# Moving start-up loads behind the first weight panels, and context steps from the expert passes to the routers and seams

## The reference, cut to what matters

```
a, ac = modulate(h, ...), modulate(hc, ...)
y, yc = swa_mixer(a, ac, ...)            # layer 2, needs the context's own output
h  = h  + gt1 * y;    h  = h  + gt2 * swiglu(modulate(h), w_gate_up, w_down)
hc = hc + gt1c * yc;  hc = hc + gt2c * swiglu(modulate(hc), w_gate_up, w_down)
y, _ = na_mixer(a, modulate(hc), ...)    # layer 3, only keys and values of the context
```

## Time and profile before

| quantity | value |
|---|---|
| median of three runs | 2652.16 us |
| profiled execution | 2653.61 us |
| its span in the trace | 2651.7 us |
| PE busy | 2322.9 us (88%) |
| DVE busy | 769.1 us (29%) |
| ACT busy | 463.2 us (17%) |
| moved by DMA | 675.05 MB, mean 255 GB/s |
| mean granted PE clock | 0.939 |

### The profile page before, as it was taken

One profiled execution on the slowest core, in us unless ns is written; L12 is line 12 of the kernel. 1 busy time (PEld: TensorE's weight loads), 2 busy tenths in 40 slices (PEclk: granted clock), 3 DMA queues, 4 the chain that ended last, 5 costly groups with the idle time before them and its releaser, 6 DMA issues.

```text
span 2651.7 us, 29654 instructions
## 1 busy us (share of the span) xinstructions
PE 2322.9 (88%) x11896; PEld 1614.3 (61%) x11896; DVE 769.1 (29%) x1935; ACT 463.2 (17%) x1156; POOL 27.7 (1%) x43
## 2 busy tenths in 40 slices
PE   5977988888997579898989989659999999989999
PEld 3643854445663247485656546337678888568888
DVE  1135335422111120843212123136810003671000
ACT  1021113321000021320000021022710002351000
POOL 0000000000000000000000000000000000110000
PEclk8999989999998889999999999879899999899999
DMA  9799288859799974809887989972024443303430
GB/s 398 313 390 371 89 364 333 368 193 421 296 401 412 421 308 159 349 1 390 342 350 277 415 347 395 421 320 96 11 97 159 152 152 126 109 23 127 149 121 16
DMA packets 94053, 675.05 MB, mean 255 GB/s; under 512 B 10833, under 2 KB 10993, under 8 KB 12385
## 3 DMA queue, kind: packets, MB, share of 16 engines
q1 hardware_dynamic: 91296, 664.84, 62.1%
q0 software_dynamic: 2048, 5.21, 0.7%
q10 hardware_dynamic: 576, 3.15, 0.3%
HBM read 672.11 MB, written 1.05 MB: 254 GB/s over the span
## 4 chain that ended last, share of the span: by engine, by line
PE 71%; DMA 15%; DVE 9%; ACT 2%; issue 2%; SPq 1%; DVEq 0%; ACTq 0%
PE bank L760 69%; DMA ring<-in_moe_w 13%; DMA ring<-in_w_ada 1%; DMA ring<-in_even_w_out 1%; DVE work L2330 1%; DVE tiny L2318 1%; DVE work L1855 1%; ACT work L1381 1%; DVE scratch L1855 1%; PE bank L1266 1%; DVE work L2341 1%; ACT res L1381 0%; ACT u L1381 0%; SPq L692 0%; ACT scratch L1381 0%
## 5 line engine op out<-in xcount | busy, mean ns | idle before, releaser
L760 PE MATMUL bank<-u,ring 128*128 128x256 f32 x2912 | 649.8, 385 | 35.0 <-ACT u L1381 22.5
L760 PEld LDWEIGHTS bank<-u,ring 128*128 128x128 f32 x2912 | 561.7, 193 | 122.8 <-issue 32.7
L760 PE MATMUL bank<-ring,work 128*32 128x512 f32 (+2 forms) x2880 | 467.6, 678 | 127.5 <-DMA ring<-in_moe_w 115.5
L760 PEld LDWEIGHTS bank<-ring,work 128*32 128x32 f32 (+2 forms) x2880 | 142.3, 130 | 408.0 <-issue 404.4
L1381 ACT ACTIVATE work<-bank 128x256 f32<-128x256 f32 (+2 forms) x150 | 73.6, 491 | 1097.4 <-PE bank L760 884.6
L760 PE MATMUL bank<-scratch,ring 128*128 128x256 f32 x1120 | 257.7, 386 | 3.0 <-ACT scratch L1381 3.0
L760 PEld LDWEIGHTS bank<-scratch,ring 128*128 128x128 f32 x1120 | 212.0, 193 | 55.2 <-issue 23.8
L760 PE MATMUL bank<-work 128*128 128x128 f32 (+3 forms) x1216 | 221.4, 337 | 26.5 <-DVE work L2234 11.4
L760 PEld LDWEIGHTS bank<-work 128*128 128x128 f32 (+2 forms) x1216 | 179.6, 198 | 63.1 <-issue 26.5
L760 PE MATMUL bank<-work,ring 128*128 128x256 f32 x704 | 152.4, 379 | 2.5 <-DVE work L2364 2.5
L760 PEld LDWEIGHTS bank<-work,ring 128*128 128x128 f32 x704 | 133.6, 190 | 21.4 <-issue 3.3
(11 more groups left out here) (235 smaller groups left out, 1743.7 us busy)
## 6 DMA issues: line engine op xcount, KB each, us to landing
ring<-in_moe_w SPq DMA_DIRECT2D x360, 1024.0 KB, 15.4
ring<-in_w_ada SPq DMA_DIRECT2D x96, 1024.0 KB, 11.3
ring<-in_w_gate_up SPq DMA_DIRECT2D x44, 1024.0 KB, 6.9
ring<-in_w_down SPq DMA_DIRECT2D x23, 1024.0 KB, 5.5
ring<-in_ctx_gate_up SPq DMA_DIRECT2D x22, 1024.0 KB, 16.2
ring<-in_even_w_in SPq DMA_DIRECT2D x14, 1024.0 KB, 10.8
ring<-in_odd_w_in SPq DMA_DIRECT2D x12, 1024.0 KB, 19.5
ring<-in_na_w_qkv SPq DMA_DIRECT2D x12, 1024.0 KB, 4.8
```

The costliest lines, as they stand in the source:

```text
L760: return pe.matmul(o, l, r, start=start, stop=stop, skip_group_check=True)
```

## The change

The constants, x and the tables `first` were issued by ACT at once, behind `cols`. Now ACT waits until the fourth slot has landed, issues const and x, and issues `first` only after its own half of `modulate(0, 0)`. x has a semaphore of its own, and `first` is waited for where it is used (PE before `sbR`, DVE before `retS`). The fifth ada job of layer 0 moves ahead of the first projection panel, and every later one moves one panel forward.

The plans: the points outside the passes hold 28 steps instead of 18. route0b and route1b go from 3 to 4, ln0b from 2 to 4, and ln1b (4) and rms2a (2) are new. The passes of layer 0 hold 56 steps instead of 63 (8 4 9 4 9 4 10 8 instead of 9 5 10 5 10 5 13 6), those of layer 1 56 instead of 59 (8 4 8 4 8 4 9 11 instead of 9 4 9 4 9 4 10 10, as only ten were left for the last pass). For ln0b, ACT and DVE now run the context's part in `odd()`, behind `modulate(1, 0)`.

```diff
-CTX_PLAN = {"even": 2, "ln0a": 2, "route0a": 2, "route0b": 3, "ln0b": 2, "ln1a": 2, "route1a": 2, "route1b": 3}
-MOE_PLAN = (("111111111", "100111010", "111211111", "100111010", "111211111", "100111010", "212211112", "212100000"),
-            ("111111111", "100101010", "111111111", "100101010", "111111111", "100101010", "112111111", "334300000"))
+CTX_PLAN = {"even": 2, "ln0a": 2, "route0a": 2, "route0b": 4, "ln0b": 4, "ln1a": 2, "route1a": 2, "route1b": 4,
+            "ln1b": 4, "rms2a": 2}
+MOE_PLAN = (("011111111", "100101010", "111111111", "100101010", "111111111", "100101010", "112111111", "332000000"),
+            ("111111110", "100101010", "111111110", "100101010", "111111110", "100101010", "401011011", "443000000"))
...
         job("adafin0a", 1)
+        ada_jobs(0, 4, 5)
         for g in range(7):
             job(f"even.{g}", 2 if g in (2, 5) else 4, panel(a["even_w_in"][0], g))
-            ada_jobs(0, 4 + g, 5 + g)
+            ada_jobs(0, 5 + g, 6 + g)
             if g >= 3:
                 ada_jobs(1, g - 3, g - 2)
-        ada_jobs(0, 11, 12)
         job("adafin0b", 1)
...
             if L == 2:
+                ctx_jobs("rms2a")
+                assert not todo, todo
+                x_banks(ALL_BANKS)
...
                 ada_sums(0, "a")
-                pe.wait_ge(first_in, 32)
+                ada(0, 4, 5)
...
                     ada(1, 4 + 3 * b, 6 + 3 * b)
                     pe.wait_ge(sb_sp, b + 1)
+                    pe.wait_ge(first_in, 16)
...
             def second(L):
                 rms_sums(f"rms{L}a", RMS_N[L][0])
+                if L == 2:
+                    ctx("rms2a")
...
             def even():
                 modulate(0, 0)
+                act.dma_start(first, a["first"]).then_inc(first_in, 16)
...
             def odd():
                 modulate(1, 0)
+                ctx("ln0b")
...
                 layer_norm(f"ln{l}b", 2, l)
-                ctx(f"ln{l}b")
+                if l:
+                    ctx("ln1b")
...
             act.dma_start(cols[:, :], a["cols"]).then_inc(cols_in, 16)
-            act.dma_start(const[:, :], a["const"]).then_inc(const_in, 16)
-            act.dma_start(x, a["x"]).then_inc(first_in, 16)
-            act.dma_start(first, a["first"]).then_inc(first_in, 16)
             act.wait_ge(cols_in, 16)
             f(cond[:, :], cols[:, 0:24], ACT.Silu).then_inc(cond_done, 1)
+            act.wait_ge(loaded[loads[3][0]], 16)
+            act.dma_start(const[:, :], a["const"]).then_inc(const_in, 16)
+            act.dma_start(x, a["x"]).then_inc(x_in, 16)
             act.wait_ge(const_in, 16)
-            act.wait_ge(first_in, 32)
+            act.wait_ge(x_in, 16)
```

More of the change, by code:

```diff
@@ L551, in build @@
         ctx_jobs("ln1b")
-        assert not todo, todo
-        x_banks(ALL_BANKS)
         for L in (2, 3):
@@ L658, in build @@
         out_done = sem("output_stored")
-        dist_in = sem("distances_loaded")
+        dist_in, x_in = sem("distances_loaded"), sem("input_loaded")
         c_sq, c_cent, c_u = sem("ctx_squares"), sem("ctx_scaled"), sem("ctx_modulated")
@@ L959, in even @@
                         project(f"even.{g}", rhs, S)
-                    ada(0, 4 + g, 5 + g)
+                    ada(0, 5 + g, 6 + g)
                     if g >= 3:
                         ada(1, g - 3, g - 2)
-                ada(0, 11, 12)
                 ada_sums(0, "b")
@@ L1889, in even @@
                 dve.wait_ge(const_in, 16)
-                dve.wait_ge(first_in, 32)
+                dve.wait_ge(x_in, 16)
                 modulate(0, 0)
-                ada(0, 4, 5)
+                ada(0, 4, 6)
                 for i in range(4):
                     copy_tile(T("even.1", i), sk[:, i], S)
-                ada(0, 5, 6)
+                ada(0, 6, 7)
                 for i in range(2):
                     copy_tile(T("even.2", i), sv[:, i], 512)
-                ada(0, 6, 7)
+                ada(0, 7, 8)
                 for i in range(4):
@@ L1901, in even @@
                 for g in range(4):
-                    ada(0, 7 + g, 8 + g)
+                    ada(0, 8 + g, 9 + g)
                     ada(1, g, g + 1)
-                ada(0, 11, 12)
                 ada_sums(0, "b")
@@ L1927, in even @@
                     ada(1, 6 + 3 * b, 7 + 3 * b)
+                dve.wait_ge(first_in, 16)
                 for h in range(4):
```

## The result

The change made the kernel **0.38% faster**: a ratio of 0.9962 with an interval of 0.9949 to 0.9974. The median of twelve executions is 2646.62 us against 2654.58 for the kernel before. The profiled executions have spans of 2644.9 and 2651.7 us, so **6.8 us less where I had forecast 24.1**. The sign is right; the size is wrong, and the time lies just outside my range. (Three single executions taken for the later runs fell in a slow state, at 3523 to 8220 us; the ratios leave them out, and they move no median by more than 0.4 us.)

The account below looks back on a forecast made before the run. Neither PE nor the DMA stream alone bounds the expert passes; they alternate. Start 2.9, layer 0 22.0 and layer 1 7.0 saved, seams 4.6 and 3.2 lost: 24.1 us less, median 2628, range 2611 to 2646.

Parts of the forecast that it names:

- The start: Kernel start: first projection 1.0 us earlier and the fifth ada job inside its wait; 2.9 us saved, bounds 0 and 4.5.
- Routers and the seams: Routers' fourth step costs nothing, leaving 0.9 us idle; seam ln0b costs 4.6 us, ln1b and rms2a 3.2.
- Layer 0, passes 0 to 3: Pass 0 brings nothing; pass 2 loses a head step, passes 1 and 3 change little: 7.4 us saved, bounds 4 and 11.
- plus 1.8 as one of two slow phases [...] goes: Layer 0, pass 2: one of two phases taking 5 to 6 us instead of 3.6 disappears, saving 1.8 us.
- rival 3: In the passes, pauses left by thirteen removed steps slow next phases on the path; 17.6 us come back: 2646, chance 0.08.
- Rival 1: The stream binds every pass, so only slots leaving the passes count, 12.5 us: 2644.6, chance 0.14.
- Layer 0, passes 4 to 7: Gather 4 to phase 5 of pass 7 takes 238.7 us instead of 253.3: 14.6 saved, bounds 5 and 25.
- Layer 1, pass 0: The pass loses its s step, worth 3.5 us less the wait for DVE's sums it filled: 2.4 us saved.
- Layer 1, passes 4 and 5: Pass 4's ring no longer restarts at once: 116.2 us from gather 4 to gather 6 instead of 105.9, 10.3 lost.
- Layer 1, pass 6: The g steps' slot frees at once, the norm stands inside, one step fewer: 64.9 us instead of 75.1, 10.2 saved.
- more than 3 us: Sign of a wrong forecast: the norm's wait in pass 6 on the path with more than 3 us.
- Layer 1, pass 7: One slot fewer to phase 5, which was 59.8 us behind its gather: 2.3 us saved.

Follow-up runs that it names:

- the start alone: The kernel before with only the diff's changes of the start, the context plan left old: 2650.35 us, ratio 0.9979.
- an even clock: Kernels before and after compared with constant products filling PE's waits by one rule in both: 2642.16 us and 2622.88 us.
- first_pair_at_0: The kernel after with both steps of the first context slot at point 0, none at g, in layer 1's passes 0, 2 and 4: 2633.03 us.
- the last column: In a dropped table, what the change gave per stretch between kernels before and after with waits filled (2642.16 and 2622.88 us); sum 19.8 us.
- before_filled: The kernel before with constant products filling head waits and waits ahead of last phases in layers 0 and 1: 2642.16 us, ratio 0.9961.
- the filled kernels: The kernel after with waits filled and layer 1's first-slot steps moved in passes 0, 2, 4: 2613.27 us; with pass 6's norm sums also earlier: 2607.33 us.
- seams_taken_back: The kernel after with the six steps of ln1b and rms2a put back into layer 1's pass 7 at point 1: 2653.96 us, ratio 0.9989.
- plan_alone: The kernel before with all the diff's changes except those of the start: 2647.45 us, ratio 0.9968.

## Why the prediction was right and wrong

- **The start** was right in kind and forecast too small: 2.9 forecast, 4.0 found at the first gather, 4.2 for the start alone, of which 3.8 reached the end. A term was missed: with one ada row less ahead of the last sums, PE's wait of 1.29 us for DVE there (ahead of the product at 163.27 in the kernel before) is gone too. Over all traces kept the first gather comes at 351.2 us on average with the old start and 345.2 with the new, so 6 us may be nearer the truth, above my bound of 4.5.
- **Routers and the seams** were right: idle time 0.94 of 0.9; the seam ln0b costs 4.4 us behind the last scatter (31.66 instead of 27.23, forecast 4.6), ln1b and rms2a cost 3.1 (first 32 products ending 106.26 us behind the left-over gather). The left-over passes of layer 0 and layers 2 and 3 gave some 2.4 and 3.3 us back, which hid it in the bare total. The 3.3 are luck: over all traces the stretch behind the left-over gather takes 955.5 us with the old seam and 957.6 with the new, 2.1 more.
- **Layer 0, passes 0 to 3: the step that failed.** The count of steps, waits and tiles was right: at an even clock passes 1 to 3 gave 5.7 us, and my 7.4 without the slow phase is 5.6 (its parts 1.6, 2.4 and 1.5 make 5.5, where I wrote 5.7). Bare they gave 0.2. What failed was "plus 1.8 as one of two slow phases [...] goes" and, in the rivals, "I take most of these phases as hidden in the wait for the stream". Of the head waits of 2.39 or 3.91 us in passes 2 to 4, all six are followed by slow work in the kernel after, three of six in the kernel before, on PE's own path; and the last phase of pass 0, which was at 3.64, takes 6.31. I had seen this as rival 3, whose place is right and whose time, 2646, is what was measured; I gave it 0.08. Its price was partly luck: some 10 us come back at an even clock (16.9 - 6.8), not the 17.6 I worked out; most of the rest of the missing 17.3 us is layer 1's, below. Rival 1, at 2644.6, is as near to the measured time, and is wrong: it lets only the bytes count, and `first_pair_at_0` gained with the same bytes in passes 2 and 4.
- **Layer 0, passes 4 to 7**: 14.6 forecast, 10.9 found to phase 5 of pass 7, 12.7 at an even clock to the next gather. Pass 4 took 64.97 us (forecast 65) and pass 5 44.85 (44.0), phase 5 of pass 6 followed its gather by 54.9 (53) and that of pass 7 came 77.7 behind it (76.7). Pass 4 has its size, the others are a little short, the most pass 6, where the norm's wait of 3.27 us is followed by slow steps.
- **Layer 1, pass 0: a term missed**, 2.4 forecast and -3.0 found. I priced the lost s step at 2.4 and overlooked what I had written down for pass 4: that a g step in an old slot lets the ring restart at once. Up8 and up9 hold the first slot until step 0 ends, the eleven others are full before that, and the stream has a hole: from SP's first expert load to phase 5 it took 73.3 us (1187.63 to 1260.92) instead of 71.2 (1196.32 to 1267.55). The last phase is slow for 2.3 more. The 1.5 in the last column says little, as this pass is 1.1 us longer in `before_filled` than in the kernel before. With its slot free earlier the pass is 3.0 us shorter than in `first_pair_at_0`.
- **Layer 1, passes 4 and 5** were right to a tenth: -10.3. (A slot is 24.83 / 10 = 2.48 us, not 2.49; nothing hangs on it.) That a context slot at g and 0 holds the whole ring is shown by `first_pair_at_0`.

The timeline of the kernel after, passes 4, 6 and 7 of layer 1, against the earlier trace rows:

```profile
1435.09 3.81 PE L762 MATMUL bank<-work 128*128 128x128 f32 x32 [0.87 <-DVE work L2243]
...
1493.04 5.34 PE L762 MATMUL bank<-ring,work 128*32 128x512 f32 x32 [3.65 <-DMA ring<-in_moe_w]
...
1551.27 3.81 PE L762 MATMUL bank<-work 128*128 128x128 f32 x32 [0.87 <-DVE work L2243]
...
1594.90 6.29 PE L762 MATMUL bank<-scratch,ring 128*128 128x256 f32 x16 [6.16 <-ACT scratch L1385]
```

- **Layer 1, pass 6**: 10.2 forecast, 7.8 found. Phase 5 of pass 4 is at +57.95 (forecast +58.0), but k3 in pass 6 waits 6.16 us for the norm, twice what layer 0's norm had shown me, and stands on the path. I had named "more than 3 us" as the sign of an error. Moving the sums earlier gave 1.6 us between the filled kernels, of the 2.4 missed here.
- **Layer 1, pass 7**: 2.3 forecast, none found. I counted slots and not their releases: the first two slots of its ring are held by pairs that are used only at g, behind the norm's steps. This is read from the trace and was not tried; `seams_taken_back` only shows that the pass answers to what stands ahead of phase 2.

## What to carry to other kernels

Work taken away from an engine that is fed by waits is not worth its length if what is left are pauses: check the granted clock behind each pause that lies on the path, and fill it with idle products whose length you have measured, shorter than the wait, and only where the trace shows a wait. Compare stretches of single traces only when you know how far two executions of the same code are apart. In a ring that is released in order, the slot that matters is the first one to be reused: put its last use ahead of everything else (both steps at g, as in pass 0), or put both uses behind slots that come free sooner (both at 0, as in passes 2 and 4).

## What the runs showed of the hardware

I had not expected that a pause of 2.39 us is enough. It doesn't always slow down what follows: ahead of the same scatter it cost nothing in the kernel before (3.62 us) and 2.5 us in the kernel after (6.14), and a wait of 5.3 us in the same trace had the same effect as one of 2.4. With 1.8 us of products in it, the remaining 0.47 us cost nothing in any head step of passes 2 to 4 (3.64, 3.62 and 7.03 us behind them, with 3.6 us in a wait of 3.91 likewise). What decides between the two cases in the bare kernels stays open. Nor is it fixed by the program alone: the head waits of layer 0 had the same outcomes in the two traces of this order of work (`plan_alone` and the kernel after), but the router's products ahead of it took 3.76 us in one execution and 6.36 in another of a program that is the same up to there.
